# The skip term of the state-space chunks, on GpSimd instead of TensorE

## What is computed

```python
def even_layer(...):
    ...
    y = ssd_scan(xh, dt, A, bm.reshape(b, s, SSD_GROUPS, SSD_STATE), cm.reshape(b, s, SSD_GROUPS, SSD_STATE))
    y = y + xh * d_skip[:, None].astype(xh.dtype)
    y = y.reshape(b, s, SSD_WIDTH) * jax.nn.silu(z)
    y_b = rmsnorm(y.reshape(b, s, SSD_GROUPS, SSD_WIDTH // SSD_GROUPS),
                  ssd_norm_w.reshape(SSD_GROUPS, SSD_WIDTH // SSD_GROUPS)).reshape(b, s, SSD_WIDTH)
```

## Time and profile before

| | us |
|---|---|
| median of three runs | 2817.12 |
| lowest, highest | 2814.34, 2817.89 |
| the profiled execution, its own time | 2814.39 |
| its span, first to last instruction | 2812.6 |
| mean granted TensorE clock | 0.961 of full |

### The profile page before, as it was taken

The page is one execution under the profiler, slowest core; times in us unless marked ns, Lnnn a source line. Parts: engine busy times, 40 slices in busy tenths (PEclk is TensorE's granted clock), DMA queues, the critical chain, the costliest instruction groups (busy, mean ns, idle before and its releaser), DMA issues. The chain is left out here.

```text
span 2812.6 us, 32482 instructions
## 1 busy us (share of the span) xinstructions
PE 2560.6 (91%) x12125; PEld 2092.3 (74%) x12125; DVE 1597.2 (57%) x2881; ACT 1217.1 (43%) x2061; POOL 202.7 (7%) x114
## 2 busy tenths in 40 slices
PE   5999598988999889899999997999599898999978
PEld 4777487867777767788888885788477686888856
DVE  6655465335555546666666664542566454666654
ACT  3555333224444433455555553431445334454432
POOL 0000021000000034000000000000232120000012
PEclk9999799999999989999999997999799998999998
DMA  2211431222121142111110100223543420111033
GB/s 103 73 68 55 147 95 58 67 90 75 53 90 51 55 135 68 38 38 38 38 36 32 38 31 15 89 97 101 181 146 113 132 85 27 40 36 45 31 120 113
DMA packets 89974, 207.05 MB, mean 74 GB/s; under 512 B 7152, under 2 KB 39792, under 8 KB 88816
## 3 DMA queue, kind: packets, MB, share of 16 engines
q1 hardware_dynamic: 89840, 205.25, 22.1%
HBM read 164.26 MB, written 40.96 MB: 73 GB/s over the span
## 5 line engine op out<-in xcount | busy, mean ns | idle before, releaser
L167 PE MATMUL acc<-operand_hi,w_hi 128*128 128x512 f32 x1830 | 742.5, 406 | 49.9 <-DVE w_lo L162 12.2
L169 PE MATMUL acc<-operand_hi,w_lo 128*128 128x512 f32 x1830 | 722.6, 395 | 0.0
L168 PE MATMUL acc<-operand_lo,w_hi 128*128 128x512 f32 x1830 | 721.2, 394 | 0.0
L167 PEld LDWEIGHTS acc<-operand_hi,w_hi 128*128 128x128 f32 x1830 | 348.8, 191 | 132.9 <-issue 37.8
L169 PEld LDWEIGHTS acc<-operand_hi,w_lo 128*128 128x128 f32 x1830 | 348.0, 190 | 76.7
L168 PEld LDWEIGHTS acc<-operand_lo,w_hi 128*128 128x128 f32 x1830 | 349.1, 191 | 69.7 <-issue 2.6
L156 ACT ACTIVATE w_hi<-w_raw 128x1024 fp32r<-128x1024 f32 (+1 forms) x209 | 202.7, 970 | 360.0 <-PE aux L169 184.3
L162 DVE TENSOR_TENSOR w_lo<-w_raw,w_hi 128x1024 fp32r<-128x1024 f32 (+1 forms) x209 | 233.1, 1115 | 217.4 <-ACT w_hi L156 217.1
L167 PE MATMUL aux<-operand_hi,w_hi 128*128 128x512 f32 x650 | 265.0, 408 | 70.3 <-DVE w_lo L162 36.5
L169 PE MATMUL aux<-operand_hi,w_lo 128*128 128x512 f32 x650 | 257.9, 397 | 0.0
L168 PE MATMUL aux<-operand_lo,w_hi 128*128 128x512 f32 x650 | 257.8, 397 | 0.0
(11 more groups left out here) (401 smaller groups left out, 4288.4 us busy)
## 6 DMA issues: line engine op xcount, KB each, us to landing
w_raw<-in_stream SPq DMA_DIRECT2D x209, 512.0 KB, 3.7
ssd_e<-cs_scratch SPq DMA_DIRECT2D x8, 1024.0 KB, 6.9
g_scratch<-conv_y SPq DMA_DIRECT2D x12, 512.0 KB, 2.9
ssd_xbc<-g_scratch SPq DMA_DIRECT2D x8, 768.0 KB, 4.7
y_scratch<-rnn_y SPq DMA_DIRECT2D x10, 512.0 KB, 3.1
out_a_raw<-y_scratch SPq DMA_DIRECT2D x20, 256.0 KB, 5.5
resid<-in_x SPq DMA_DIRECT2D x8, 512.0 KB, 7.6
g_scratch<-mlai_g SPq DMA_DIRECT2D x8, 512.0 KB, 2.9
```

Of the source, the lines that this page charges most:

```text
L167: pe.matmul(out, w_hi, x_hi, start=first, stop=False)
L168: pe.matmul(out, w_hi, x_lo, start=False, stop=False)
L169: return pe.matmul(out, w_lo, x_hi, start=False, stop=last)
```

## The change

dg and the eight products with it are gone, and each product L2370 now starts and ends its own accumulation. POOL multiplies xs by d_skip itself. In chunk 0, where nothing is carried, the result goes straight into yy. In the later chunks it goes back into xs, and a second POOL instruction adds it to yy, behind a wait for both halves of the carried part (y1). DVE adds px and yy in every chunk, behind a wait for s["skip"]. ACT's copy into xs waits for the skip term of the chunk before in place of its xdt.

```diff
-                pe.wait_ge(s["dg"], 1)
-                for t in range(DT):
-                    pe.matmul(px[:, t * P:(t + 1) * P], x[:, t, :], dg[:, t, :], start=True, stop=False)
-                    for n in (2 * t, 2 * t + 1):
-                        d = slice(n * HD, (n + 1) * HD)
-                        mm = pe.matmul(px[:, d], e[:, b % 2, n, :], xdt[:, d], start=False, stop=n % 2 == 1)
+                for n in range(SSD_HEADS):
+                    d = slice(n * HD, (n + 1) * HD)
+                    mm = pe.matmul(px[:, d], e[:, b % 2, n, :], xdt[:, d], start=True, stop=True)
                 mm.then_inc(s["yd"], 1)
...
                 if b:
-                    act.wait_ge(s["xdt"], b)
+                    act.wait_ge(s["skip"], b)
                 act.activation(xs[:, :], px, ACT.Copy).then_inc(s["xs"], 1)
...
-            d = k.row[:, ROW["d_skip"]:ROW["d_skip"] + SSD_HEADS].rearrange("p (t e) -> p t e", e=2)
-            pool.tensor_tensor(dg[:, :, :].rearrange("p t (e l) -> p t e l", l=HD),
-                               k.ident[:, :].rearrange("p (e l) -> p e l", l=HD).unsqueeze(1).to_broadcast([P, DT, 2, HD]),
-                               d.unsqueeze(3).to_broadcast([P, DT, 2, HD]), ALU.mult).then_inc(s["dg"], 1)
+            d = k.row[:, ROW["d_skip"]:ROW["d_skip"] + SSD_HEADS].unsqueeze(2).to_broadcast([P, SSD_HEADS, HD])
...
                     pool.tensor_tensor(heads(hd[:, :]), heads(h[:, :]), head_col(b, 4), ALU.mult).then_inc(s["hd"], 1)
+                if not b:
+                    pool.wait_ge(s["in_z"], 16)
+                    pool.tensor_tensor(heads(yy[:, 0, :]), heads(xs[:, :]), d, ALU.mult).then_inc(s["skip"], 1)
+                else:
+                    pool.tensor_tensor(heads(xs[:, :]), heads(xs[:, :]), d, ALU.mult).then_inc(s["xd"], 1)
+                    pool.wait_ge(s["xd"], b)
+                    pool.wait_ge(s["y1"], 2 * b)
+                    pool.tensor_tensor(yy[:, b % 2, :], yy[:, b % 2, :], xs[:, :], ALU.add).then_inc(s["skip"], 1)
...
                 dve.wait_ge(s["yd"], b + 1)
-                if b:
-                    dve.wait_ge(s["y1"], 2 * b)
-                    dve.tensor_tensor(y, px, y, ALU.add).then_inc(s["y2"], 1)
-                else:
-                    dve.tensor_copy(y, px).then_inc(s["y2"], 1)
+                dve.wait_ge(s["skip"], b + 1)
+                dve.tensor_tensor(y, px, y, ALU.add).then_inc(s["y2"], 1)
```

More of the change, by code:

```diff
@@ L2191, in ssd_chunks @@
     k.tile += DT
-    s = k.sems("ssd", "in_x0 in_x1 in_z in_c0 in_c1 tx tz tb cb xs btok tanh zs cbm xdt xdd e1 e2 e g hd h yo st yd y1 y2 yy dg "
+    s = k.sems("ssd", "in_x0 in_x1 in_z in_c0 in_c1 tx tz tb cb xs btok tanh zs cbm xdt xdd e1 e2 e g hd h yo st yd y1 y2  yy xd skip "
                       "sq v sd rms yn turned yt stored in_y0 in_y1 in_y2 yhi ylo first added")
@@ L2198, in ssd_chunks @@
         xbc, e = sb("xbc", [P, 2, CONV_TILES, P]), sb("e", [P, 2, SSD_HEADS, P])
-        zc, dg = sb("zc", [P, Z_TILES, P]), sb("dg", [P, DT, P])
+        zc = sb("zc", [P, Z_TILES, P])
         xs, xdt, xdd, h, hd, yt = (sb(n, [P, S]) for n in "xs xdt xdd h hd yt".split())
```

## The result

The changed kernel takes 2835.45 us, median of 4 runs (2831.15 to 2836.43), the kernel before 2815.73 in the runs beside it. The ratio is 1.0065, 95% interval 1.0052 to 1.0077. It is slower, by 15 to 22 us, and inside the range that was forecast (2825 to 2853). The profiled execution has a span of 2834.6 us, 22.0 more than before.

A forecast was written before the change was run, and what follows sets the result against it. The prediction took a loop through TensorE and VectorE, which has 0.31 us to spare, as the bound. 1.7 + 5 x (1.8 + 2.3) = 22.2 us gave 2836.6, or 2839 us as median; range 2825 to 2853.

The forecast's parts named there:

- The loop goes through DVE: Middle chunks: PE waits for DVE's L2514, so 1.79 us less PE work gains only 0.3 us per chunk.
- The spare time of DVE: Middle chunks: DVE's part of the loop has 0.31 us idle before the addition L2514.
- The dependencies are covered: Middle chunks: POOL's new multiplication (1.90 us) and addition (2.39 us) fit before DVE needs the result at 2062.5.
- DVE and POOL exclude each other, small steps too: Middle chunks: L336 stands during POOL's addition, 2.1 us late; net +1.8 us per chunk for b = 2 to 6.
- The rival in which the small steps pass: L336 to L338 and L2534 lose less than 0.3 us beside POOL: 2817 us, no difference; chance 0.08.
- the scaling beside POOL: If small steps passed, scaling L2534 would stand: about 1.5 instead of 1.8 us per chunk, 2838 us in all.
- The clock: Middle chunks: after a 3.6 us PE gap the clock drops to half, costing 2.3 us per chunk (ends 0 and 4.6).
- The rival in which the clock holds: No low clock behind the 3.6 us gaps in chunks 2 to 6: 10.7 us more, 2828 us; chance 0.18.
- the one in which it stays low over all 4.6 us: Half clock over all of PE's serial part in middle chunks: 33.7 us more, 2851 us; chance 0.10.
- Edges: Chunk 0: L2543 stands behind POOL's product, +1.7 us; chunks 1 and 7 taken at 0, between -0.3 and +2.
- The sum: Whole kernel: 1.7 + 5 x (1.8 + 2.3) = 22.2 us over the profiled 2814.39, median 2839 us.
- the upper end: Top of the forecast range: low clock with 2.4 instead of 2.1 us of DVE delay, 2853 us.

The follow-up runs named there:

- e1_pe_only: Kernel before with the eight dg products removed from TensorE and nothing put in their place on GpSimd: 2807.63 us, ratio 0.9966.
- e2_no_add: Changed kernel without GpSimd's addition to yy in chunks 1 to 7, its multiplication of xs kept: 2810.31 us, 0.9983 of the kernel before.
- e7_before_order: Kernel before, skip term on TensorE, with small steps and scalings done early, xdt behind the mask product, hd a chunk earlier: 2812.41 us, ratio 0.9986.
- e3_no_mult: Changed kernel without GpSimd's multiplication of xs by d_skip in chunks 1 to 7, its addition kept: 2834.30 us, 1.0070 of the kernel before.
- e4_pe_kept: Changed kernel with dg and TensorE's eight products put back, so the skip term is added twice: 2824.70 us, 1.0033 of the kernel before.
- e6_skip0_late: Changed kernel with chunk 0's GpSimd product of xs and d_skip waiting until chunk 1's differences are done: 2832.16 us, one run.

## Why the prediction was right, point by point

- **The loop goes through DVE.** Shown by e1_pe_only: 1.79 us less work on PE shorten the chunk by 0.56. The spare time of DVE, a term of 0.3 us in the sum, measured 0.56. L2514 (L2516 in the changed kernel) starts right behind the product with the gate and gains 0.4 us. L2580 seems to have stood for PE as well, which I had not counted: from the start of the weight split to its own start 1.30 us passed before (2061.29 to 2062.59) and 1.14 us in the changed kernel (2092.22 to 2093.36).
- **The dependencies are covered.** The multiplication is free in the middle chunks (e2_no_add), and ACT and POOL show no new wait there. Only in chunk 7, which has no hd, POOL's addition waits 3.7 us for y1.
- **DVE and POOL exclude each other, small steps too.** Forecast 2.1 us, measured 2.15 (L336 at 2.31 for 0.16). With the larger spare time the net is +1.55 instead of +1.8 per chunk. The rival in which the small steps pass is refuted. What the prediction says of the scaling beside POOL was not met by any row of L2534, but L2530, a TENSOR_SCALAR as well, stood beside POOL in e7_before_order.
- **The clock.** Right in kind, too large in size: 2.3 us were taken, between the 1.6 and 2.97 of the two stops of the earlier trace rows; 1.4 were measured. This is the term that was sized worst. The stop was 3.27 us long, not 3.6, because DVE's net delay was 1.55 and not 1.8; behind it the clock was at 0.50 for 3.41 us, as for 3.21 us behind the stop of 3.37, and not for 5.94 as behind the one of 3.77. The forecast 3.6 lay a little nearer to 3.77, so nothing in the rows could have chosen the short stretch, and the middle was a guess. The length of the stop alone does not settle it either: in e3_no_mult five stops of 3.30 us were followed by about 7 us at 0.50 once and by 3.4 us four times. The rival in which the clock holds (2828 us) is refuted by the rows at 0.50 and by e4_pe_kept; the one in which it stays low over all 4.6 us (2851 us) by PE's 6.00 us for that part, where it would take 9.2.
- **Edges.** Chunk 0 cost 1.7 us, as forecast, and e6_skip0_late shows the cause. Chunks 1 and 7, taken at 0, gained 0.7 and 0.2 us. The gain in chunk 1 lies outside the bounds of -0.3 and +2 and does not come from the products that TensorE lost: e4_pe_kept, which has them, gains as much (29.25). In both the low clock in chunk 1 lasts about 7 us instead of 10.3, as in e1_pe_only; the cause stays open.
- **The sum.** In the stage 15.7 us against 22.2 forecast: the clock's 5 x 0.9 is the larger part of the error, the spare time's 5 x 0.25 and the edges' 0.9 the rest. The medians differ by 19.7 us, nearer to the forecast than the stage is. The 4 us between lie outside the stage, where nothing was changed, and their cause is not known, so it is partly luck that the total came so close to 2839: in the stage the measured 15.7 is nearer to the 10.7 of the rival in which the clock holds than to 22.2. What speaks for the forecast are the single steps, not the total. One sum was off by a little: the upper end by its own terms is 1.7 + 5 x (2.1 + 4.6) = 35.2, so 2852 and not 2853.

## What to carry to other kernels

Before work goes to GpSimd, write down what VectorE does at that moment: an instruction there with two SBUF operands that comes while GpSimd's is running stood until its end in this kernel, even with two numbers per partition, and so did a small TENSOR_SCALAR. So put the new one beside VectorE's PSUM reads or its idle time. Follow the loop through every engine before counting TensorE's saving, since TensorE at 97% of a chunk had another engine half a microsecond behind it. And when a saving on TensorE turns into a stop of some three microseconds, count the half clock behind that stop as well: stops of 3.3 us brought it in each middle chunk and one of 2.4 us did in e6_skip0_late, stops of 0.4 to 1.6 us at this place did not.

## What was not expected of the hardware

The low-clock stretches of the changed kernel begin 27.30 to 27.31 us apart, from 2068.80 to 2178.02, one in each of chunks 2 to 6 and each 3.41 us long; here are the first and the last.

```profile
2068.80:2072.21 3.41, 2.90 (x7) 2.33 (x8) 0.62 (x2) 3.39 (x7) 0.00 (x0) 0.50 0.42 171
...
2178.02:2181.43 3.41, 3.13 (x7) 2.49 (x8) 0.39 (x2) 3.39 (x6) 0.00 (x0) 0.50 0.19 62
```

The chunks' lengths drift from 27.19 to 27.31 us, and PE's busy time at the half clock grows from 2.90 to 3.13 us meanwhile. It looks as if the chunks drew into step with the stretches. e3_no_mult is not in step: there too the stretches of chunks 3 to 6 begin 27.3 us apart and last 3.4 us, while these chunks take 27.48 to 27.51 us. The stretches begin 1.2 us behind the end of PE's stop in chunk 3 and 0.6 us behind it in chunk 6, where those of the changed kernel begin 0.3 to 0.5 us before it, and PE is busy for the whole 3.41 us. So what a stretch costs depends on how much of PE's work lies in it, and a loop with such a stop in every round may take small savings back. This was only observed; what sets the distance of the stretches was not tested.
